# Seven block products in place of eight for four column blocks of gate and up in each feed-forward layer

## What is computed

```python
def swiglu(x, w_gate, w_up, w_down):
    return (jax.nn.silu(x @ w_gate) * (x @ w_up)) @ w_down
```

## Time and profile before

| | |
|---|---|
| median of three runs | 1620.4 us (1619.58 to 1620.77) |
| profiled execution, first to last instruction | 1618.1 us |
| TensorE busy | 1609.3 us, 99% |
| VectorE busy | 957.4 us, 59% |
| ScalarE busy | 776.3 us, 48% |
| GpSimd busy | 78.7 us, 5% |
| mean DMA rate | 190 GB/s, 306.77 MB in all |
| mean granted clock of TensorE | 0.999 |

### The profile page before, as it was taken

One profiled execution on the slowest core, in us unless ns is written; L12 is line 12 of the kernel. 1 busy time (PEld: TensorE's weight loads), 2 busy tenths in 40 slices (PEclk: granted clock), 3 DMA queues, 4 the chain that ended last, 5 costly groups with the idle time before them and its releaser, 6 DMA issues.

```text
span 1618.1 us, 18458 instructions
## 1 busy us (share of the span) xinstructions
PE 1609.3 (99%) x7791; PEld 1342.0 (83%) x7791; DVE 957.4 (59%) x959; ACT 776.3 (48%) x815; POOL 78.7 (5%) x104
## 2 busy tenths in 40 slices
PE   9999999999999999999999999999999999999998
PEld 7888897788888888888988888888888998888886
DVE  6555466676554775455668545565446657685553
ACT  7444447655443764442656434354443436454340
POOL 0121000000000000001010000000000131000000
PEclk9999999999999999999999999999999999999999
DMA  9856474466654866563647546666555554576560
GB/s 319 231 179 208 157 240 140 163 198 219 192 187 131 276 205 185 159 221 98 237 158 253 182 156 211 204 201 188 161 206 182 196 178 148 182 241 188 162 216 26
DMA packets 222097, 306.77 MB, mean 190 GB/s; under 512 B 8896, under 2 KB 144320, under 8 KB 221888
## 3 DMA queue, kind: packets, MB, share of 16 engines
q1 hardware_dynamic: 217232, 290.29, 55.4%
q0 software_dynamic: 4416, 15.05, 2.9%
q10 hardware_dynamic: 368, 0.27, 0.1%
HBM read 304.52 MB, written 1.05 MB: 189 GB/s over the span
## 4 chain that ended last, share of the span: by engine, by line
PE 99%; DVE 0%; DMA 0%; SPq 0%; ACT 0%; issue 0%; DVEq 0%
PE bank L696 29%; PE bank L709 29%; PE bank L700 26%; PE bank L646 3%; PE bank L713 3%; PE bank L773 2%; PE bank L775 2%; PE bank L776 2%; PE bank L1117 0%; PE bank L907 0%; DMA raw<-in_ffn_w_up 0%; PE bank L926 0%; PE bank L916 0%; PE bank L1054 0%; PE bank L759 0%; PE bank L1136 0%
## 5 line engine op out<-in xcount | busy, mean ns | idle before, releaser
L1614 DVE TENSOR_TENSOR low<-raw,hiw 128x2048 fp32r<-128x2048 f32 (+2 forms) x296 | 631.4, 2143 | 382.9 <-ACT hiw L1229 381.9
L1229 ACT ACTIVATE hiw<-raw 128x2048 fp32r<-128x2048 f32 (+1 forms) x280 | 521.8, 1871 | 358.1 <-DMA raw<-in_ffn_w_out 87.9
L696 PE MATMUL bank<-hiw,xh 128*128 128x512 f32 x1404 | 384.9, 396 | 0.0
L709 PE MATMUL bank<-low,xh 128*128 128x512 f32 x1404 | 376.3, 390 | 0.0
L700 PE MATMUL bank<-hiw,xl 128*128 128x512 f32 x1232 | 330.1, 390 | 0.0
L709 PEld LDWEIGHTS bank<-low,xh 128*128 128x128 f32 x1404 | 263.2, 188 | 55.8 <-DVE low L1614 0.2
L696 PEld LDWEIGHTS bank<-hiw,xh 128*128 128x128 f32 x1404 | 257.1, 188 | 52.5 <-issue 2.8
L700 PEld LDWEIGHTS bank<-hiw,xl 128*128 128x128 f32 x1232 | 231.2, 188 | 49.6
L696 PE MATMUL bank<-hiw,th 128*128 128x512 f32 x524 | 143.7, 392 | 0.0
L700 PE MATMUL bank<-hiw,tl 128*128 128x512 f32 x524 | 142.2, 389 | 0.0
L709 PE MATMUL bank<-low,th 128*128 128x512 f32 x524 | 142.1, 389 | 0.0
(11 more groups left out here) (276 smaller groups left out, 1177.9 us busy)
## 6 DMA issues: line engine op xcount, KB each, us to landing
raw<-in_ffn_w_in SPq DMA_DIRECT2D x176, 512.0 KB, 4.9
raw<-in_ffn_w_out SPq DMA_DIRECT2D x40, 1024.0 KB, 5.0
raw<-in_ret_w_in SPq DMA_DIRECT2D x24, 1024.0 KB, 5.1
raw<-in_ffn_w_gate SPq DMA_DIRECT2D x42, 512.0 KB, 4.3
raw<-in_ffn_w_up SPq DMA_DIRECT2D x42, 512.0 KB, 5.3
raw<-in_ffn_w_down SPq DMA_DIRECT2D x20, 1024.0 KB, 5.1
raw<-in_w_in SPq DMA_DIRECT2D x16, 1024.0 KB, 5.7
raw<-in_gla_w_in SPq DMA_DIRECT2D x12, 1024.0 KB, 5.2
```

Source lines behind the costliest of these rows:

```text
L696: pe.matmul(o[:, :], tokens(0, k), whi[:, k, :], start=start and k == 0, stop=False, skip_group_check=True)
L709: ins = pe.matmul(o[:, :], tokens(0, k), wlo[:, k, :], start=False, stop=end, skip_group_check=True)
L1229: act.activation(hiw[s][:, 0:n], raw[s][:, 0:n], ACT.Copy).then_inc(hi.mark(i), 1)
L1614: dve.tensor_tensor(low[s][:, c0:c1], raw[s][:, c0:c1], hiw[s][:, c0:c1].bitcast(F32), ALU.subtract).then_inc(lo.mark(*what), 1)
```

## The change

Of the 11 column blocks of a feed-forward layer, blocks 3 and 4 and blocks 7 and 8 are taken as pairs. For a pair, the left side is the 2 x 2 block matrix of tokens (a11, a12 for tokens 0 to 127, a21, a22 for 128 to 255, each with half of the 1024 columns) and the right side that of the weights (b11, b21 for the first column block, b12, b22 for the second). Before, this is eight block products of 12 matmuls, two for each of the four results. After, it is seven (Winograd's form of Strassen's scheme): a11 b11, a12 b21, s0 t1, s1 t2, s2 t3, s3 b22 and a22 t4, up to signs, with four sums of tokens (s0 to s3) and four of weights (t1 to t4).

- The token sums are made once a layer by VectorE in fp32, in `dve_token_sums`: the whole `x` from its two parts (`xs`), four sums of 128 x 512, then a split into high (ScalarE, `sh`, 128 x 2048) and low (VectorE, `sl`, 128 x 2048).
- The weight sums are made for each pair by VectorE (`dve_weight_sums`), four of 128 x 2048, each just before the low part of the tile that precedes its use. t1, t2 and t4 have no load of their own; t3 is made in place.
- All seven right sides are split into high and low, where four weight tiles were split before.
- The results come together in two banks, bank 6 and bank 7: ScalarE copies three partial results out (u1, s5, u2, 128 x 512 each), later products go on adding in the same bank, and VectorE adds the copies to the banks three times (`added`, 128 x 512), before silu and the multiplication in halves.
- The seven slots become 14 single blocks (12 in f1 and f2). High parts, loads and sums take blocks one by one (`give_blocks`), the high part four tiles ahead of use, a load six. `ahead` looks at all blocks that a tile and its sums need.
- The steps of a layer stand in one list, `FFN_STEPS`, which all three engines follow; plain tiles stand between the products, and turns are moved.

What is loaded from memory is the same, in a slightly other order (`load_key`). The down product, the mixers and the norms are unchanged but for the names of the blocks. The core of the diff:

```diff
+LOAD_LEAD, HIGH_LEAD = 6, 4
+SUMS = ("t1", "t2", "t3", "t4")
+FFN_PAIRS = (3, 7)
+FFN_STEPS = (
+    ("tile", 0, 0), ("tile", 0, 1), ("tile", 1, 0), ("tile", 1, 1), ("turn", 0),
+    ("token sums",),
+    ("product", 0, "b11"), ("tile", 2, 0), ("blocks",), ("tile", 2, 1), ("turn", 1),
+    ("product", 0, "t1"), ("tile", 5, 0),
+    ("product", 0, "t2"), ("tile", 5, 1), ("turn", 2),
+    ("product", 0, "b22"), ("product", 0, "t3"), ("tile", 6, 0), ("p",),
+    ("product", 0, "b21"), ("turn", 4), ("product", 0, "t4"), ("tile", 6, 1), ("turn", 5),
+    ("product", 1, "b11"), ("turn", 3), ("tile", 9, 0),
+    ("product", 1, "t1"), ("product", 1, "t2"), ("tile", 9, 1), ("turn", 6),
+    ("product", 1, "b22"), ("product", 1, "t3"), ("tile", 10, 0),
+    ("product", 1, "b21"), ("turn", 8), ("product", 1, "t4"), ("tile", 10, 1), ("turn", 9), ("turn", 7))
...
         def ahead(i):
 
             j = i
-            while j + 1 < NT and j < i + 5 and freed_by[j + 1] <= i - 2:
+            while j + 1 < NT and j < i + 5 and needed[j + 1] <= i - 2:
                 j += 1
             return j
...
+        def pe_product(pe, i, xh_of, xl_of, o, start):
+
+            whi, wlo = weight(i)
+            pe_hi(pe, i)
+            for k in range(4):
+                pe.matmul(o[:, :], xh_of(k), whi[:, k, :], start=start and k == 0, stop=False, skip_group_check=True)
+            for k in range(4):
+                pe.matmul(o[:, :], xl_of(k), whi[:, k, :], start=False, stop=False, skip_group_check=True)
+            pe_lo(pe, i)
+            for k in range(4):
+                ins = pe.matmul(o[:, :], xh_of(k), wlo[:, k, :], start=False, stop=k == 3, skip_group_check=True)
+            ins.then_inc(passed.mark(i, 1), 1)
...
+                elif m == "t1":
+                    if g == 0:
+                        pe.wait_ge(fn.sem, fn.of("sh", name))
+                        pe.wait_ge(vec.sem, vec.of("sl", name))
+                    else:
+                        pe.wait_ge(vec.sem, vec.of("c11", name, g - 1))
+                    pe_product(pe, grp[g].t1, *s_block(f, 0), bank[7], True)
...
+            if m == "b11":
+                freed(dve, load_after[g.t1])
+                loaded(g.b11)
+                loaded(g.t3)
+                dve_sum(dve, g.t1, g.t3, g.b11)
+            elif m == "t1":
+                freed(dve, load_after[g.t2])
+                loaded(g.b22)
+                dve.wait_ge(vec.sem, vec.of("sum", g.t1))
+                dve_sum(dve, g.t2, g.b22, g.t1)
...
+            def added(g, i, copy, dst, o, what):
+                dve.wait_ge(passed.sem, passed.of(i, 1))
+                dve.wait_ge(fn.sem, fn.of(copy, name, g))
+                dve.tensor_tensor(dst, o[:, :], dst, ALU.add).then_inc(vec.mark(what, name, g), 1)
...
+                if m == "b22":
+                    added(g, grp[g].b22, "u2", u2, bank[7], "c12")
+                    times(u2[:, 256:512], u2[:, 256:512], u2[:, 0:256], second, 0)
...
+                elif step == "product":
+                    dve_lows(dve, ahead(spot[(name, *what)]))
+                    product(*what)
```

More of the change, by code:

```diff
@@ L220, in build @@
             rsl = sb("rsl", [P, 4, 384], F32R, ar)
[L221 to L224, removed]
+        weight_block()
+        weight_block()
         with ExitStack() as ar:
@@ new lines, in give_blocks @@
+        def give_blocks(first, end, among):
+            events = []
+            for i in range(first, end):
+                if tiles[i].pieces:
+                    events.append((load_key[i] - LOAD_LEAD, "load", i))
+                events.append((i - HIGH_LEAD, "high", i))
+            for g in group.values():
+                if first <= g.b11 < end:
+                    for of, i in ((g.b11, g.t1), (g.t1, g.t2), (g.t2, g.t4)):
+                        events.append((of + 0.6 - HIGH_LEAD, "sum", i))
+            for _, what, i in sorted(events):
+                b = min(among, key=lambda m: block_age[m][0])
+                if what == "high":
+                    high_to[i], high_after[i] = b, block_age[b]
+                else:
+                    load_to[i], load_after[i] = b, block_age[b]
+                block_age[b] = (i, None)
@@ L1228, in act_high @@
                 else:
[L1229 removed]
+                    act.activation(split[s][:, 0:n], whole[r][:, 0:n], ACT.Copy).then_inc(hi.mark(i), 1)
         def act_turned(act, key, dst):
@@ L1843, in dve_ffn @@
                 turn(0)
[L1844 to L1850 removed]
+                steps = FFN_STEPS[LEAD_STEPS:]
+            for step, *what in steps:
+                if step == "tile":
+                    j, n = what
+                    if name == "f1" and j == 0:
+                        dve_lows(dve, 4)
+                    else:
+                        dve_lows(dve, ahead(spot[name, j, n]))
+                    if n:
+                        mult(j, 0)
+                        mult(j, 1)
+                elif step == "turn":
+                    turn(*what)
+                elif step == "token sums":
+                    dve_token_sums(dve, f)
+                elif step == "blocks":
+                    dve.wait_ge(fn.sem, fn.of("sh", name))
+                    dve.tensor_tensor(f.sl[:, :, :, :], f.sx[:, :, :, :], f.sh[:, :, :, :].bitcast(F32),
+                                      ALU.subtract).then_inc(vec.mark("sl", name), 1)
+                elif step == "product":
+                    dve_lows(dve, ahead(spot[(name, *what)]))
+                    product(*what)
+                elif step == "p" and name == "f2":
                     dve.wait_ge(fn.sem, fn.of("ph"))
```

411 lines of the change are left out of this document (292 added, 119 removed).

## The result

The changed kernel takes 1639.12 us (median of four runs, 1637.44 to 1639.99) beside 1620.23 on the same chip: the ratio is 1.0115, 95% interval 1.0103 to 1.0127. It is slower by 1.15%, where 0.6% faster was forecast, and outside the range. The profiled execution spans 1637.7 us, 19.6 more than that of before.

What follows compares the result with a forecast made beforehand. TensorE bounded the kernel; after the change VectorE would set the pace. Four layers at -3.2 and two at +1.7 us give -9.4 on the profiled 1618.1, so 1608.7, or 1611 for the median; range 1598 to 1617, chance 0.55.

Steps and rivals of the forecast that it cites:

- Removed work: 144 matmuls fewer on TensorE save 32.6 us; its own time per stretch falls from 102.33 to 96.89 us.
- The price of a weight sum: Each 128x2048 weight sum on VectorE was taken at 2.21 us, with bounds of 2.21 to 2.76.
- The walk: Engine orders followed through blocks 2 to 10: stalls 2.2 us in layers with 14 blocks, 7.1 in f1 and f2.
- the bubbles: VectorE's waits around the multiplication in steps with an addition: about 0.45 us before it, 1.6 behind it.
- Rival C: VectorE's hand-overs to ScalarE in the pairs cost 3.3 us more per layer, giving 1631 us; chance 0.14.
- rival B: TensorE stays the bound, stalls under 1 us a layer; 1590 us or so, up to 1597; chance 0.13.
- The price of a pause: TensorE's stalls in the stretches were counted at their length alone, 2.2 or 7.1 us a layer.
- rival D: After the stall at t1, 12 matmuls run at 0.45 us, 2.7 us per layer, giving 1627; chance 0.05.
- The rule that the prediction named: Idle gaps between matmuls send TensorE back to half clock; the trace was silent for gaps of 1 to 3 us.
- DMA: I cost it at nothing: Loads under the new block allocation cost nothing: the lead in the pairs is 15 us and more, a load lands in 4.9.
- the prediction's own sign: If TensorE's idle time names ScalarE's high part or a DMA, the walk's order is wrong.
- the centre of the matter: In the rebuilt stretch VectorE gets 97.0 us of work against TensorE's 96.9, and must still wait for other engines.

Runs made afterwards that it cites:

- e12: e9 with the low parts of t2, t3 and t4 left out on VectorE, TensorE's matmuls the same in number and order; 1600.47 us.
- e2: Changed kernel with whole slots again for the last six down tiles of f2 and a1 and the tiles behind them; 1622.56 us.
- e5: e2 with pairs only in the four layers with 14 blocks, f1 and f2 plain as before the change; 1615.42 us.
- e10: e5 with b0's down tiles in whole slots and nine matmuls on zeros before TensorE's wait for the split token sums; 1609.00 us.
- e1: Changed kernel with whole slots again for the last six down tiles of f2 and the tiles behind them; 1627.64 us.
- e7: e2 with products t1 and t2 of the first pair later, each behind a plain tile; 1630.02 us.
- e4: e2 without VectorE's 48 weight sums, loaded weight tiles standing in for them; 1621.85 us.
- e9: As e8, but t1 and t2 stand together behind tile 5.0; 1622.28 us.
- e6: e2 with only the first pair, blocks 3 and 4, in each layer; 1638.02 us.
- e3: e2 with nine matmuls on zeros before TensorE's wait for the split token sums in each layer; 1624.22 us.
- e8: e5 with the later t1 and t2 of e7 and the old allocation behind b0's down product; 1619.12 us.

## Why the prediction was wrong

The forecast was -9.4 us in the profile; +19.6 came. The 29.0 us between them, by its own steps:

**Removed work: right.** 96.89 us for a stretch without stalls; e12 shows 96.85. The price of a weight sum was right too, 2.296 us (bound 2.21 to 2.76), and 48 of them as said:

```profile
L1820 DVE TENSOR_TENSOR whole<-whole 128x2048 f32<-128x2048 f32 x48 | 110.2, 2296 | 0.0
```

VectorE's busy time was forecast at 1206 and is 1196.0, ScalarE's 874 and 860.0. TensorE's was forecast at 1577 and is 1591.0, since a matmul at the lower clock or right behind a pause counts as busy for longer. Its idle time, the span less the busy time, is 46.7 us, where 32 were forecast: 13.3 more are the three pauses at the edges (7.85, 4.16 and 1.29) and 2.3 those at the start.

**The walk: right to a few tenths in the four layers with 14 blocks, in f1 and f2 near only in its sum.** VectorE of after in a1, where u = 0 is 897.35:

```profile
911.19 2.29 DVE L2136 TENSOR_TENSOR sl<-sx,sh 128x2048 fp32r<-128x2048 f32 x1
...
935.73 0.69 DVE L2099 TENSOR_TENSOR xn<-bank,xn 128x512 f32<-128x512 f32 x1
936.90 0.43 DVE L2090 TENSOR_TENSOR xn<-xn 128x256 f32<-128x256 f32 x1 [0.48 <-ACT xn L1509]
938.71 2.29 DVE L1816 TENSOR_TENSOR split<-whole,split 128x2048 fp32r<-128x2048 f32 x1 [1.38 <-ACT split L1384]
940.92 0.68 DVE L2099 TENSOR_TENSOR xn<-bank,xn 128x512 f32<-128x512 f32 x1
...
987.06 0.43 DVE L2090 TENSOR_TENSOR xn<-xn 128x256 f32<-128x256 f32 x1 [0.48 <-ACT xn L1509]
```

c12 begins at u = 38.4 (the walk said 38.5), c22 at 43.6 (43.8), the last multiplication at 89.7 (89.3); the bubbles are 0.48 and 1.38 (0.45 and 1.6). `sl` ends at 16.1 (15.5). So TensorE pauses there (the row calls it issue; the matmul starts 0.1 us behind the end of `sl`) and at turn 8 for

```profile
913.58 1.17 PE L846 MATMUL bank<-split,sh 128*128 128x512 f32 x4 [1.90 <-issue]
...
987.54 0.66 PE L734 MATMUL bank<-ident,xn 128*128 128x128 f32 x4 [0.53 <-DVE xn L2090]
```

2.4 us against 2.2, and the stretch is 99.67 against 99.1. In f1 and f2 the pauses are 6.9 and 5.8 us against 7.1, at the places that the walk named, but not in its sizes: f1 has 0.76 at t1 where 3.2 were forecast, and 2.40 at turn 8 where it was 0.8. That its sum comes out is in part luck. Those of f2, as far as over 1 us, and the largest of f1:

```profile
398.99 1.20 PE L851 MATMUL bank<-split,sh 128*128 128x512 f32 x4 [2.28 <-DVE split L1816]
...
439.87 1.19 PE L846 MATMUL bank<-split,xh 128*128 128x512 f32 x4 [1.30 <-DVE xn L2087]
...
129.37 0.66 PE L734 MATMUL bank<-ident,xn 128*128 128x128 f32 x4 [2.40 <-DVE xn L2087]
```

Over the six stretches the pauses are 22.4 us, 23.0 were forecast (4 x 2.2 + 2 x 7.1). Rival C is thereby refuted. In rival B one sum was off: 1587.8 + 6 is 1593.8 and not 1590; the forecast didn't use it.

**The price of a pause: the second step that failed, 9.8 us.** The stretches take 614.2 us where 604.4 were forecast, and it isn't the length of the pauses. TensorE's own work is 581.2 (6 x 96.86) and the pauses 22.4, which leaves 10.6 us that the sum priced at nothing. Its work and pauses together were 0.8 too long, hence 9.8. TensorE of after in a0, behind the same pause as in a1:

```profile
624.22 1.15 PE L846 MATMUL bank<-split,sh 128*128 128x512 f32 x4 [1.91 <-issue]
625.21 1.64 PE L848 MATMUL bank<-split,sl 128*128 128x512 f32 x4
626.64 1.91 PE L851 MATMUL bank<-split,sh 128*128 128x512 f32 x4
628.35 1.35 PE L784 MATMUL bank<-split,xh 128*128 128x512 f32 x4
```

The clock fell to its lower level, 0.428 us a matmul from 626.64 on. This is rival D, with other sizes: it costs 1.6 us in a0 and b1 (against a1 and b0) and not 2.7, it came in four of six layers (f1, f2, a0, b1), and in f1 it came behind the pause at turn 8 and not at t1. The other part is the restart: in a1, 99.67 less 96.85 of work and 2.43 of pauses leaves 0.39 for two, so 18 pauses at about 0.2 are 3.5 of the 10.6 us and the four falls some 7. Two more fell at the edges. The rule that the prediction named from the Trainium skill, "TensorE: Matmul & The Clock Gate", Part 1 (idle gaps between matmuls send the array back to half clock), thus holds here, but not every time: the same 1.9 us pause at t1 led to the lower level in two of four such layers in after, in none in e2, in three in e5. The page tells it of waits that are longer than these, and of short ones that come often, so that rival D didn't follow from it for single pauses of 1 to 3 us, as the prediction put it; the runs decide, and they show it there too. That the pause is what matters is shown by e10, in which it is filled and no clock falls.

**"DMA: I cost it at nothing": the first step that failed, 17.1 us.** The term is the one for the new allocation: how long a load, or a high part, waits for the block it is given. It was argued for the gate-and-up part, with places between a tile and the one whose block it takes, and there it holds: no pause of TensorE in the six stretches is put down to a transfer. It wasn't asked of the tiles of the next stage, which take blocks of down tiles d8 to d11 whose t = 1 pass stands at the layer's end. Two places fewer meant 19 us less of lead. e1 and e2 show it, each by giving one edge its old slots: -9.5 and -6.0. No rival had this step; the prediction's own sign, idle time that names a DMA, is what ScalarE's row has. At f2 it was a load that came late, at a1 a high part that waited for its block.

For the 1.7 us behind b0 what is late is of the same kind, but the allocation isn't shown to be the cause. In after, ScalarE makes seven high parts there 2.6 to 2.7 us apart and each but the first waits some 0.8 us for its load; the last, ahead of the norm, begins 49.7 us behind the start of the down product. In before it is 44.1, in e7 43.9 and in e10 45.0, and there TensorE has no pause. In all the runs the pauses behind the down products of a0, a1 and b0 come where this last high part begins 49.7 us or more behind the start of the down product, also behind a0 in e4, e9 and e12; where there is no pause, it is 45.2 or less. But the loads of the retention mixer's first tiles wait for the same down tiles before and after the change, and with the change's allocation the 1.7 us are missing in e4, e6 and e7 and there in e1, e2, e3 and e5. Why the loads come late in some of them stays open.

**The start**, 2.1 us: a later first load of `h` (a pause of 1.21 in place of 0.17) and a pause of 1.26 at the turn of block 0 in f1, where a low part stands ahead of VectorE's multiplication. With plain f1 (e5) the start is back, u = 0 at 31.67. The pause for `h` varies from run to run, between 0.21 and 1.30 us in most, and with plain f1 too (0.21 in e5, 0.75 in e8), so the change isn't shown to be its cause.

17.1 + 9.8 + 2.1 = 29.0. Had the edges alone been kept, as in e2, the forecast of 1611 would still have been missed by 11.6 us; in its profiled execution, 10.4 above the forecast 1608.7, 6.6 are in the six stretches, 1.9 behind b0 and 1.8 at the start.

That the amount of VectorE's work is the centre of the matter was right, but only partly the reason: at t1 it is a chain of hand-overs (e4), behind it the amount of work on top of such waits (e12).

## What to carry to other kernels

A change that takes other buffers must be followed to the first tiles of the next stage: ask of each what it takes over and when that is used for the last time, by time and not by places in the list. Matmuls saved by sums of operands are paid on VectorE, and a pause of TensorE that comes of it costs its length, 0.2 us for the restart, and at times 1.6 more; where it can't be removed, filling it (e10) was worth more than moving it (e7 to e9). Use such a scheme only where the look-ahead is long enough: the stretches of the four layers with 14 blocks gained 11.2 us in e10, the two with 12 lost 7.8 in the change.

## What the runs showed of the hardware that I had not expected

- A pause of 1.9 us between matmuls was followed by matmuls at the 1.2 GHz level, with 1.6 us lost, in some layers and by full pace in others, in the same execution and with the same instructions ahead of it. The runs' times spread with it: 5.0 us in e5 and 7.4 in e2, where the granted clock of the whole run is 0.998 at 1618.97 us and 0.994 at 1626.35; but 0.3 in e10 and 0.1 in e12, whose rebuilt stretches have no pause over 0.6 us, and 1.2 in the kernel before. Pauses don't always do it: e7, with pauses of 2.3 us, spread by only 0.4. What decides it stays open.
- Nine matmuls of unused bf16 data in the gap were enough, and delayed the product that followed by nothing that can be seen (605.13 in e10, 605.08 in e5).
- VectorE sets the pace of TensorE at 90.4 us busy in 99.67: nearly all of the rest is 13 hand-overs with ScalarE of 0.23 to 1.38 us, 8.9 us in all in a1's stretch.
